# Sums of squares between layers: additions in place on VectorE, one matmul on the total, three blocks on a half's rows

## The reference

```python
def _rmsnorm(x, g):
    y = xf * lax.rsqrt(jnp.mean(xf * xf, axis=-1, keepdims=True) + RMS_EPS)
    return (y * g.astype(jnp.float32)).astype(x.dtype)
...
    for i in range(DEPTH):
        h = _rmsnorm(hres, norm_g[i, 0])
        m = ...                                 # attention (i = 0) or short convolution (i = 1)
        hres = hres + _rmsnorm(m, norm_g[i, 1])
        h = _rmsnorm(hres, norm_g[i, 2])
        hres = hres + _rmsnorm(_sqrelu_mlp(h, w_up[i], w_down[i]), norm_g[i, 3])
```

## Time and profile before

| | us |
|---|---|
| median of 3 runs (lowest to highest) | 1647.27 (1646.14 to 1649.56) |
| profiled execution | 1647.33 |
| its span | 1645.5 |

### The profile page before, as it was taken

One profiled execution on the slowest core, in us unless ns is written; L12 is line 12 of the kernel. 1 busy time (PEld: TensorE's weight loads), 2 busy tenths in 40 slices (PEclk: granted clock), 3 DMA queues, 4 the chain that ended last, 5 costly groups with the idle time before them and its releaser, 6 DMA issues.

```text
span 1645.5 us, 31409 instructions
## 1 busy us (share of the span) xinstructions
PE 1566.9 (95%) x12656; PEld 1404.8 (85%) x12656; DVE 785.6 (48%) x1368; ACT 620.9 (38%) x1135; POOL 530.4 (32%) x235
## 2 busy tenths in 40 slices
PE   7999998999999999999999999999999989999895
PEld 6898988999999999999989888888889867777764
DVE  4444443744232231565446642332316799566655
ACT  5566664443232232432224532322324534433321
POOL 3222222044444444134430344444441244450010
PEclk9999999999999999999999999999999999999998
DMA  5121121222222322222222222323222222200001
GB/s 183 53 65 52 53 65 52 65 90 90 90 91 93 99 92 90 78 77 90 91 88 78 77 90 93 100 90 100 92 92 76 64 81 87 90 16 3 3 27 51
DMA packets 35401, 125.66 MB, mean 76 GB/s; under 512 B 3920, under 2 KB 4048, under 8 KB 35280
## 3 DMA queue, kind: packets, MB, share of 16 engines
q1 hardware_dynamic: 35280, 123.90, 23.5%
HBM read 121.79 MB, written 2.10 MB: 75 GB/s over the span
## 4 chain that ended last, share of the span: by engine, by line
PE 70%; DVE 11%; issue 2%; ACT 2%; DVEq 0%; ACTq 0%
PE G L1419 59%; PE G L1689 3%; PE ST L1689 2%; PE ST L1392 2%; PE PV L1689 1%; PE PO L1689 1%; DVE rstd L867 1%; DVE acc L1323 1%; DVE wlo L906 1%; DVE t L1173 0%; DVE z L1176 0%; DVE m L926 0%; ACT rms L535 0%; DVE z L1165 0%; PE PO L1419 0%
## 5 line engine op out<-in xcount | busy, mean ns | idle before, releaser
L462 POOL TENSOR_TENSOR wlo<-raw,whi 128x1024 fp32r<-128x1024 f32 x209 | 507.1, 2427 | 1073.7 <-ACT whi L511 632.9
L1419 PE MATMUL G<-xh,whi 128*128 128x258 f32 (+3 forms) x1504 | 372.0, 310 | 11.7 <-DVE t L1012 6.9
L1419 PE MATMUL G<-xl,whi 128*128 128x258 f32 (+3 forms) x1504 | 358.6, 301 | 0.0
L1419 PE MATMUL G<-xh,wlo 128*128 128x258 f32 (+3 forms) x1504 | 356.8, 300 | 0.0
L1419 PE MATMUL G<-ah,whi 128*128 128x256 f32 (+2 forms) x1024 | 278.5, 313 | 4.7 <-DVE al L1148 2.9
L1419 PE MATMUL G<-al,whi 128*128 128x256 f32 (+2 forms) x1024 | 276.9, 311 | 0.0
L1419 PE MATMUL G<-ah,wlo 128*128 128x256 f32 (+2 forms) x1024 | 276.9, 311 | 0.0
L521 ACT ACTIVATE whi<-raw 128x1024 fp32r<-128x1024 f32 x112 | 118.7, 1060 | 418.8 <-PE G L1419 414.7
L1419 PEld LDWEIGHTS G<-xh,whi 128*128 128x128 f32 x1504 | 244.4, 189 | 30.5 <-issue 11.5
L1419 PEld LDWEIGHTS G<-xh,wlo 128*128 128x128 f32 x1504 | 244.9, 189 | 9.7
L1419 PEld LDWEIGHTS G<-xl,whi 128*128 128x128 f32 x1504 | 243.8, 189 | 10.7
(11 more groups left out here) (306 smaller groups left out, 2021.0 us busy)
## 6 DMA issues: line engine op xcount, KB each, us to landing
raw<-weights_dram SPq DMA_DIRECT2D x225, 512.0 KB, 3.5
hres<-xT_dram SPq DMA_DIRECT2D x8, 264.0 KB, 6.2
out_dram<-hres SPq DMA_DIRECT2D x8, 256.0 KB, 2.1
con<-consts_dram SPq DMA_DIRECT2D x1, 512.0 KB, 7.4
mat<-mats_dram SPq DMA_DIRECT2D x1, 512.0 KB, 8.2
con<-consts_dram SPq DMA_DIRECT2D x1, 392.0 KB, 5.7
vec<-vecs_dram SPq DMA_DIRECT2D x1, 203.0 KB, 2.5
```

What stands on the lines that cost most here:

```text
L462: nc.gpsimd.tensor_tensor(wlo[:, s], raw[:, s % 2], whi[:, s].bitcast(F32), ALU.subtract)\
L1419: last_of[0] = nc.tensor.matmul(to[:, p0:p1], wt[:, w, ws], xt[:, k, t0 - off:t1_ - off], start=k == 0 and q == 0, stop=k == KT - 1 and q ...
```

## The change

- The square of an input row goes in place of the row's scaled product output in `m` (`squared_row`), no longer to a slot of `t1`; ScalarE's wait for `sq_used` goes.
- VectorE adds the squares of rows 1 to 6 of a half to that of row 0 (`add_row`, from row 3 on after each `low_x`), and TensorE takes two matmuls per half, one on the total and one on row 7 (`row_total`), in place of eight.
- In the first half blocks 0, 1 and 2 take the rows (block 2 rows 0 to 3 in one go, then all three blocks row by row), and block 3 follows; the sum of the last product's norm comes after block 2's first four rows. In the second half blocks 0 and 1 take the rows, block 2's first two rows go in after row 3.
- VectorE: the reciprocal of the new norm for the first half moves behind the second half's rows; that of the last product's second half moves behind `low_w(new + 3)`. ScalarE: the first half's square root of the new norm moves behind row 2 of the second half.
- The fifth block of a product waits for one tile less where its number is a constant (the products of 8 blocks), and the MLP evicts tiles 0 and 1 ahead of the first `low`.

```diff
@@ squares and roots on ScalarE
+        def squared_row(k, cols, half):
+            return m[:, k, tokens(cols, half, cols[0])]
...
-                if s % 2 == 0:
-                    act.wait_ge(sq_used, sq_base(s) + KT * ((half or 0) + 1))
+                if s == 0:
+                    act.wait_ge(sq_used, KT)
+                elif s % 2 == 0:
+                    act.wait_ge(sum_joined, s - 2 + half + 1)
...
-                    c = tokens(cols, half)
-                    if k + KT * half >= 4:
-                        act.wait_ge(sq_used, sq_base(s) + KT * half + k - 3)
-                    r, o = square_slot(k, half)
-                    nc.scalar.activation(t1[:, r, o:o + c.stop - c.start], hres[:, k, c], ACT.Square).then_inc(sq_ready, 1)
+                    nc.scalar.activation(squared_row(k, cols, half), hres[:, k, tokens(cols, half)], ACT.Square)\
+                        .then_inc(sq_ready, 1)
...
-                stat_root(s, cols, 0)
                 for k in range(KT + 2):
                     input_row(k, 1)
+                    if k == 2:
+                        stat_root(s, cols, 0)
@@ last_tiles on VectorE
+                def add_row(k, half):
+                    n = 6 * (2 * i + half) + k
+                    dve.wait_ge(sq_ready, sq_base(s + 1) + KT * half + k + 1)
+                    if k >= 2:
+                        dve.wait_ge(row_added, n - 1)
+                    total = squared_row(0, cols, half)
+                    nc.vector.tensor_tensor(total, total, squared_row(k, cols, half), ALU.add).then_inc(row_added, 1)
...
                         if k >= 1:
                             low_x(i + 1, *pre, k - 1, cols, half)
+                        if k >= 3:
+                            add_row(k - 2, half)
...
                 input_rows((6, 7), 0)
+                low_x(i + 1, *pre, KT - 1, cols, 0)
+                add_row(6, 0)
+                low_w(new + 3)
                 stat_recip(s, cols, 1)
-                low_x(i + 1, *pre, KT - 1, cols, 0)
-                low_w(new + 3)
-                stat_recip(s + 1, cols, 0)
                 dve.wait_ge(rstd_ready, stat_count(s, 1))
                 scaled(0, 1)
                 input_rows(range(KT), 1)
                 low_x(i + 1, *pre, KT - 1, cols, 1)
+                add_row(6, 1)
+                stat_recip(s + 1, cols, 0)
                 stat_recip(s + 1, cols, 1)
@@ mlp on VectorE
-                                up(b0 + UP[c] + j, j, (b0 + UP[c] + j) % 4)
+                                if j != 1:
+                                    evict(b0 + UP[c] + j, j, (b0 + UP[c] + j) % 4)
+                                if j == 0:
+                                    evict(b0 + UP[c] + 1, 1, (b0 + UP[c] + 1) % 4)
+                                low(j, (b0 + UP[c] + j) % 4)
@@ TensorE
+            def row_total(s, cols, half):
+                (_, _, p0, p1), = part(cols, half)
+                pe.wait_ge(rms_ready, stat_count(s - 1, half))
+                pe.wait_ge(row_added, 6 * (s - 2 + half + 1))
+                nc.tensor.matmul(ST[:, p0:p1], ones, squared_row(0, cols, half), start=True, stop=False, skip_group_check=True)
+                pe.wait_ge(sq_ready, sq_base(s) + KT * (half + 1))
+                nc.tensor.matmul(ST[:, p0:p1], ones, squared_row(KT - 1, cols, half), start=False, stop=True,
+                                 skip_group_check=True).then_inc(sum_joined, 1)
...
-            def begin(b):
+            def begin(b, fifth=False):
                 pe.wait_ge(lo_ready, b + 1)
                 if not isinstance(b, int) or b >= 2:
-                    pe.wait_ge(tile_out, b - 1)
+                    pe.wait_ge(tile_out, b - (2 if fifth else 1))
...
+                for k in range(KT // 2):
+                    ready(k, 0)
+                    rows(0, [k], 0)
+                    rows(1, [k], 0)
+                start(2)
+                rows(2, range(KT // 2), 0)
+                post_stat(s - 1, cols, 1)
+                for k in range(KT // 2, KT):
+                    ready(k, 0)
+                    for j in range(3):
+                        rows(j, [k], 0)
+                start(3)
+                rows(3, range(4), 0)
+                row_total(s, cols, 0)
+                rows(3, range(4, KT), 0)
+                for k in range(KT):
+                    ready(k, 1)
+                    for j in range(2):
+                        rows(j, [k], 1)
+                        if k == KT - 1:
+                            done()
+                    if k == 3:
+                        if cols[1] - cols[0] > BANK:
+                            pe.wait_ge(rms_ready, stat_count(s, 0))
+                        rows(2, range(2), 1)
+                rows(2, range(2, 6), 1)
+                row_total(s, cols, 1)
+                rows(2, range(6, KT), 1)
+                done()
+                if cols[1] - cols[0] > BANK:
+                    pe.wait_ge(rms_ready, stat_count(s, 1))
+                rows(3, range(KT), 1)
+                done()
```

More of the change, by code:

```diff
@@ L126, in half_added @@
     return j + 1 + (HELD - 1 if half else 0)
-def square_slot(k, half):
-    q = k + KT * half
-    return q % 2, TOK // 2 * (q // 2 % 2)
 def held(cols, j, half):
@@ L252, in program @@
         sqr_ready = sem("sqr_ready")
+        row_added = sem("row_added"); sum_joined = sem("sum_joined")
         lam_prod = sem("lam_prod"); lam_exp = sem("lam_exp"); lam_ready = sem("lam_ready")
@@ L534, in stat_root @@
                 pieces = part(cols, half)
-                nc.scalar.activation(rms[:, tokens(cols, half)], ST[:, pieces[0][2]:pieces[-1][3]], ACT.Sqrt, scale=1.0 / D,
-                                     bias=eps_t[:, 0:1]).then_inc(rms_ready, 1)
+                nc.scalar.activation(rms[:, tokens(cols, half)], ST[:, pieces[0][2]:pieces[-1][3]], ACT.Sqrt,
+                                     scale=1.0 / D, bias=eps_t[:, 0:1])\
+                    .then_inc(rms_ready, 1)
             def post_squares(b0, i, cols, layer, n):
@@ L1001, in low, with evict @@
                                 .then_inc(a_ready, 1)
-                        def up(b, j, s4):
+                        def evict(b, j, s4):
                             dve.wait_ge(block_done, b + 1)
@@ L1015, in up @@
                             last.then_inc(tile_out, 1)
+                        def up(b, j, s4):
+                            evict(b, j, s4)
                             low(j, s4)
@@ L1380, in _, with first_sum @@
         def _(pe):
-            def stat_tile(s, k, cols, half=None):
-                if k == 0 and s >= 1:
-                    pe.wait_ge(rms_ready, stat_count(s - 1, half))
-                pe.wait_ge(sq_ready, sq_base(s) + KT * (half or 0) + k + 1)
-                for t0, t1_, p0, p1 in part(cols, half):
-                    if s == 0:
-                        squares = sq[:, k % 2, t0:t1_]
-                    else:
-                        r, o = square_slot(k, half)
-                        squares = t1[:, r, o:o + t1_ - t0]
-                    last = nc.tensor.matmul(ST[:, p0:p1], ones, squares, start=k == 0, stop=k == KT - 1,
+            def first_sum(k):
+                pe.wait_ge(sq_ready, k + 1)
+                for t0, t1_, p0, p1 in part(ALL):
+                    last = nc.tensor.matmul(ST[:, p0:p1], ones, sq[:, k % 2, t0:t1_], start=k == 0, stop=k == KT - 1,
                                             skip_group_check=True)
                 last.then_inc(sq_used, 1)
+            def row_total(s, cols, half):
[6 more added lines that the diff above has]
+                                 skip_group_check=True).then_inc(sum_joined, 1)
             def post_stat(s, cols, half=None):
@@ L1440, in start @@
                     pe.wait_ge(tile_out, b0 + j - 3)
-                for half in range(2):
-                    if half == 0:
-                        start(0)
-                        start(1)
-                    for k in range(KT):
-                        pe.wait_ge(x_ready, x_base(i + 1) + KT * half + k + 1)
-                        if k >= 2:
-                            stat_tile(s, k - 2, cols, half)
-                        for j in range(2):
-                            rows(j, [k], half)
-                            if half and k == KT - 1:
-                                last_of[0].then_inc(block_done, 1)
-                        if k == 4 and half == 0:
-                            post_stat(s - 1, cols, 1)
-                    stat_tile(s, KT - 2, cols, half)
-                    stat_tile(s, KT - 1, cols, half)
-                    for j in range(2, HELD):
-                        if half == 0:
-                            start(j)
-                        else:
-                            pe.wait_ge(rms_ready, stat_count(s, j - 2))
-                        rows(j, range(KT), half)
-                        if half:
-                            last_of[0].then_inc(block_done, 1)
@@ new lines, in ready, with done @@
```

(12 more changed lines are left out.)

## The result

The changed kernel takes **1674.35 us** (median; 1666.57 to 1676.72) against 1647.76 for the kernel before, run beside it: ratio 1.0153, 95% interval [1.0139, 1.0168]. The direction was forecast; the loss is 26.6 us where 20.8 was forecast. The profiled execution of after is the longest of its four, 1676.72 with a span of 1674.9, so distances in its trace add up to 29.4 us. The four executions took 1676.72, 1675.38, 1673.32 and 1666.57 us at mean granted clocks of 0.979, 0.984, 0.983 and 0.988: the 10 us between them go largely with the clock.

A forecast was written before the change was run, and what follows sets the result against it. TensorE bounds the kernel except in four seams (normalise, add residual, form next product's input), where the last reciprocal's start decides; 16.3 us from seams plus 4.5 of clock on 1647.33 gave 1668 us, range 1658 to 1680.

The forecast's parts named there:

- clock rival: Each seam's first half: TensorE's clock also falls after the idle ahead of block 2; 4 to 7.6 us more, chance 0.24.
- Part 1: Seams: 48 of 64 summing matmuls leave TensorE, 20.6 us, a gain only where TensorE is what ends last.
- Part 2: VectorE's six additions per half: each stalls 0.58 us for its square, a row taking 2.04 us instead of 1.13.
- Part 3: A seam's first half: TensorE idles 3.0 us ahead of block 2; the second half starts 1.2 us later.
- Part 4: A seam's second half: the last reciprocal starts 5.8 us later in each seam.
- What a seam makes of it: Product block after each seam's idle starts later: +2.1, +5.8, +2.6 and +5.8 us in seams 1 to 4, sum 16.3.
- The clock: Low clock after idle ahead of block 5: 1.8 us for seams 2 and 3, half for seam 1, sum 4.5.
- rival without stalls: VectorE's additions find squares ready, cost only 0.33 us each; last reciprocal +0.4, seams -5.2, total 1642; chance 0.08.
- TensorE is the bound throughout: Whole kernel: the 20.6 us of removed summing matmuls come off whole, 1627; chance 0.02.

## Why the prediction was right, and where its sizes were off

The measured 1674.35 lies in the stated range of 1658 to 1680, above the forecast's own band (1661 to 1672) and in that of its clock rival (1672 to 1680).

- **Part 1** held: 48 matmuls left, and none of their 20.6 us reached the total, since with the stalls VectorE's rows end last.
- **Part 2** held: 2.04 us a row, a stall of 0.57 where 0.58 was read. Without the stall (additions one row later) 26 of the 26.6 us are gone.
- **Part 3** held up to block 2, which starts 17.04 us into the seam, forecast 315.7 - 298.67 = 17.0; the idle time ahead of it is 2.63 us for the 3.0 forecast. Behind it the step failed: it took the sum of the last norm at full clock, so the addition of row 5 at 1.1 us of wait. It was 2.31. With TensorE kept busy (work in the gap) it is 1.10. So the mechanism was the right one; the mis-sized term is the root's lateness, by 1.2 us.
- **Part 4** was right in its working: 5.7 and 5.8 us where the clock was kept. The trace of after has 7.2 to 7.9. The first half's clock is 1.4 to 1.6 of this (the old eviction order, seams 3 and 4 over 1 and 2: 1.4; seam 4 of after, with no low clock in its second half: 7.24). The second half's low clock is the other 0.6, and 1.1 in the kernel with work in the gap.
- **What a seam makes of it** held in kind: block 5 waits in seams 1 and 3, and the chained seams 2 and 4 pass the whole shift on (7.7 of 7.9, 7.2 of 7.2). In seam 1 the fourth tile was put down at +0.1 and came 0.9 later than that: from last reciprocal to block 5 it is 13.13 us (355.79 - 342.66), forecast 12.2. The prediction let evictions and squares alternate as before and left out the splits in ScalarE's queue and GpSimd's subtractions behind them. Of the 0.9 the traces put 0.5 down to the third tile's squares (9.17 us after the last reciprocal's start, 8.64 in before) and 0.4 to its low part beside GpSimd (1.91 us for 1.53). With 2.0 from the reciprocal that makes 5.0 for the forecast 2.1. It is not the same in each execution: with the gap filled it was 12.55.
- **The clock** was sized well as an episode (1.8, measured 1.7), but not in number. The rival "the clock falls in the first halves too", priced at 4 to 7.6 us more and given 0.24, came true in all four seams of the profiled execution; measured against the run with the gap filled it costs 5.4 us (7.0 by the distances to their own kernels before). It explains nearly all of the 5.8 by which the forecast was short, and the forecast without it (1668, 20.8 us over before) is what that run took (1669.0, 19.6 over its own). The low clock behind block 5 was forecast at 4.5 us and came to 5.1, but seam by seam (0.9, 1.8, 1.8, 0 against 1.5, 0.0, 2.6, 1.0) the agreement is luck. In seam 2 the episode came (0.57 in 746 to 750), but an episode of before (0.50 in 850 to 852) has none to match it in after (1.00 in 848 to 854). The chance was too low: three idle gaps of four in before spoke for it. The rule of the Trainium skill, "TensorE: Matmul & The Clock Gate", section "Why this matters for your kernels", that long idle gaps between bursts be avoided since the clock then drops, pointed the right way. The runs here show it as a tendency: of the eight first halves with an idle time of 2.5 to 2.7 us (after and the kernel with the old evictions) six had the low clock. Of the 24 in the six kernels in which that idle time is shorter or filled, none had it.
- **The rival without stalls** had its seams right and its total wrong: shift 0.3 (forecast 0.4), seams -5.1 (forecast -5.2), but 1648.2 and not 1642. It left out the low clock behind block 5's wait in seams 1 and 3, which the forecast's own sum had counted. A term that stands in the forecast has to be asked for in every rival.
- *TensorE is the bound throughout*, 1627, is refuted: without the additions the kernel still takes 1638.9. The run with the moved reciprocal alone shows the true part of it: in the second half of before TensorE ended last, since VectorE could end its rows 3.4 us sooner with no effect.

What stays open is why the clock falls in one seam and not in another of the same kernel. What after loses behind block 5 is the low clock too as far as the stretches go: 0.79 and 0.50 in 356 to 360 of seam 1, which is 1.4 of the 1.5 us, and 0.50 to 0.52 from 952 to 958 of seam 3, some 5.5 us from block 5's start at 952.47 on, which is 2.7 us for the 2.6. What makes the 1.0 us of seam 4 stays open too.

## What to carry to other kernels

Work moved from a full engine to a half-idle one costs its wait, not its duration: an addition of 0.33 us cost 0.9 because its operand was made one step too late by an engine that itself waits for the adder, and one row of distance paid the whole loss back. Look in each in-order queue for work ahead of the critical instruction that could stand behind it, whether it waits for something (the late sum: 5.2 and 5.6 us) or only takes its time and starts another engine that gets in the way (the splits: 2.7 and 8.7, or 3.6 and 7.7 by the distances to their own kernels before). A short idle time of TensorE can cost as much again in clock, so compare it with what useful work could fill it.

## What the runs showed of the hardware

- Useless work made the kernel faster: 20 matmuls in a gap of 2.63 us kept the granted clock at 1.00, where it had been 0.55 and 0.59, and 5.4 us of the total came back.
- An idle time of 2.63 us was followed by the low clock in seam 1 of after and not in seams 1 and 2 of the kernel with the old evictions; 2.74 was not in seam 2 of before. Executions of one kernel can thus differ by 1.7 us for each such episode, and the four of after lie 10 us apart.
- VectorE's low part, of two operands in SBUF, takes 0.69 us alone (341.16 above) and 1.98 while GpSimd's subtraction runs: it starts at 348.59, GpSimd's ends at 347.60 + 2.42 = 350.02, and VectorE's ends 0.55 later. In after 62 of the 64 low parts of this kind start while GpSimd subtracts, and every one ends 0.55 us after it. The Trainium skill, "SBUF — State Buffer", section "SBUF: two separate sides", states that a VectorE instruction with two inputs in SBUF and a GpSimd instruction that reads SBUF share a pair of ports under an exclusive lock: whichever starts first has it for its whole instruction, and the other is blocked. These rows agree.
